# An encoder kernel on TensorE: where the first transposed piece of a step stands among the scores and the projection

## The reference

```python
h = rms_norm(x, g)
z = h @ w_in                       # q, k, v of both kinds of heads, and a gate
o = concat(diff_attention(...),    # 4 heads, each with two softmaxes over all 1024 keys
           neighbourhood_attention(...))   # 8 heads over an 8 x 16 neighbourhood
x = x + (o * silu(gate)) @ w_out
```

## Time and profile before

| what | value |
|---|---|
| time, median of 3 runs | 1527.56 us (1527.29 to 1528.21) |
| the profiled execution | 1533.38 us |
| its span | 1531.5 us |
| TensorE busy | 1458.8 us, 95% |
| VectorE busy | 908.7 us, 59% |
| ScalarE busy | 699.3 us, 46% |
| mean granted clock of TensorE | 0.98 of full speed |

### The profile page before, as it was taken

The page is one execution under the profiler, slowest core; times in us unless marked ns, Lnnn a source line. Parts: engine busy times, 40 slices in busy tenths (PEclk is TensorE's granted clock), DMA queues, the critical chain, the costliest instruction groups (busy, mean ns, idle before and its releaser), DMA issues. The chain is left out here.

```text
span 1531.5 us, 24892 instructions
## 1 busy us (share of the span) xinstructions
PE 1458.8 (95%) x8288; PEld 1192.9 (78%) x8288; DVE 908.7 (59%) x1892; ACT 699.3 (46%) x1338; POOL 507.3 (33%) x498
## 2 busy tenths in 40 slices
PE   7899999999999999899999999999999999997995
PEld 6687887878787878678887878788878888876874
DVE  6467676767555555663436766767665555557323
ACT  5345554555444444442515555545444444454330
POOL 2233333243423232302643242423252323331261
PEclk9899999999999999899999999999999999998996
DMA  6500101111111201301210111001111111122012
GB/s 197 119 29 22 48 21 34 34 44 50 36 52 42 58 34 58 131 15 42 69 42 28 36 35 34 21 31 37 53 42 53 42 51 41 51 70 82 28 55 110
DMA packets 39249, 79.45 MB, mean 52 GB/s; under 512 B 18832, under 2 KB 18832, under 8 KB 39184
## 3 DMA queue, kind: packets, MB, share of 16 engines
q1 hardware_dynamic: 39184, 78.60, 16.5%
HBM read 66.57 MB, written 15.96 MB: 54 GB/s over the span
## 5 line engine op out<-in xcount | busy, mean ns | idle before, releaser
L877 PE MATMUL proj<-h_hi,w_hi 128*128 128x512 f32 x1184 | 504.4, 426 | 31.0 <-DVE h_lo L1371 13.7
L879 PE MATMUL proj<-h_hi,w_lo 128*128 128x512 f32 x1184 | 469.6, 397 | 0.0
L878 PE MATMUL proj<-h_lo,w_hi 128*128 128x512 f32 x1184 | 466.4, 394 | 0.0
L877 PEld LDWEIGHTS proj<-h_hi,w_hi 128*128 128x128 f32 x1184 | 224.8, 190 | 106.5 <-issue 61.7
L879 PEld LDWEIGHTS proj<-h_hi,w_lo 128*128 128x128 f32 x1184 | 224.3, 189 | 52.3
L878 PEld LDWEIGHTS proj<-h_lo,w_hi 128*128 128x128 f32 x1184 | 225.9, 191 | 34.6
L1281 DVE CUSTOM_DVE_ANT_0 prob<-scores,inner 128x1024 f32<-128x1024 f32 (+1 forms) x192 | 204.2, 1063 | 50.0 <-PE scores L913 47.2
L1289 DVE TENSOR_TENSOR pt_lo<-turn,pt_hi 128x512 fp32r<-128x512 f32 (+1 forms) x208 | 138.8, 667 | 147.2 <-ACT pt_hi L746 146.7
L557 POOL TENSOR_TENSOR w_lo<-w_raw,w_hi 128x1024 fp32r<-128x1024 f32 x78 | 188.7, 2419 | 109.3 <-ACT w_hi L704 109.2
L746 ACT ACTIVATE pt_hi<-turn 128x512 fp32r<-128x512 f32 (+1 forms) x208 | 120.7, 580 | 225.0 <-PE turn L970 225.0
L772 ACT ACTIVATE prob<-prob,nm,escale_now 128x1024 f32<-128x1024 f32 x128 | 158.2, 1236 | 0.4 <-DVE nm L1285 0.4
(11 more groups left out here) (159 smaller groups left out, 2226.8 us busy)
## 6 DMA issues: line engine op xcount, KB each, us to landing
w_raw<-chunks SPq DMA_DIRECT2D x81, 512.0 KB, 3.4
mixed_dram<-gate SPq DMA_DIRECT2D x28, 256.0 KB, 2.3
edge<-bias_dram SPq DMA_DIRECT2D x32, 224.0 KB, 3.8
h_lo<-mixed_dram SPq DMA_DIRECT2D x14, 512.0 KB, 7.1
xt<-x_t SPq DMA_DIRECT2D x8, 512.0 KB, 9.4
bias_dram<-bias_rows SPq DMA_DIRECT2D x16, 240.0 KB, 6.1
out_t<-prob SPq DMA_DIRECT2D x6, 512.0 KB, 3.0
out_t<-gate SPq DMA_DIRECT2D x2, 512.0 KB, 3.0
```

Of the source, the lines that this page charges most:

```text
L877: pe.matmul(dst, a_hi, b_hi, start=start, stop=False)
L878: pe.matmul(dst, a_hi, b_lo, start=False, stop=False)
L879: return pe.matmul(dst, a_lo, b_hi, start=False, stop=stop)
```

## The change

TensorE's step: before, the piece of projection was cut into three parts of 2, 3 and 3 contraction steps, and the first transposed piece stood between the first two. Now the first transposed piece stands directly behind the scores, and the projection fills in parts of 5 and 3. In the last group of a layer the slots of `LAST_FILL` are taken two, one and one. VectorE's step in a DA group: the low part of the first piece now stands between the two `shifted`, not behind both. In an NA group VectorE's order stays; in the last group the additions of slot 0 move behind the first `p_part`.

```diff
-                    parts = [range(0, 2), range(2, 5), range(5, 8)]
-                    if last_step:
-                        parts = [range(0, 2), range(2, 5), range(5, 8), ()]
+                    parts = [range(0, 5), range(5, 8), ()]
 
                     def fill(j):
-                        if not behind and LAST_FILL[t] and j < len(LAST_FILL[t]):
-                            for p, ks in LAST_FILL[t][j]:
-                                out_piece(g.l, p, ks)
+                        if not behind:
+                            for slot in LAST_FILL[t][(0, 2, 3)[j]:(2, 3, 4)[j]]:
+                                for p, ks in slot:
+                                    out_piece(g.l, p, ks)
                         if front and front.projects(ft):
                             group_piece(front, ft, parts[j])
 
+                    turn_p(g, t - 1, 0)
                     fill(0)
-                    turn_p(g, t - 1, 0)
-                    fill(1)
                     turn_p(g, t - 1, 1)
                     if g.na and INNER[t - 1]:
                         turn_p(g, t - 1, 2)
-                    fill(2)
+                    fill(1)
...
             def attend(g, behind):
                 for t, front, ft in steps(g, behind):
-                    if front:
-                        for m in range(2):
-                            shifted(front, ft, m)
...
+                    if front:
+                        shifted(front, ft, 0)
+                    if not g.na:
+                        p_part(g, t - 1, 0)
+                    if front:
+                        shifted(front, ft, 1)
                     for c in range(3 if g.na and INNER[t - 1] else 2):
-                        if c < 2:
-                            add_pieces(c)
-                        p_part(g, t - 1, c)
+                        if c == 1:
+                            add_pieces(0)
+                            add_pieces(1)
+                        if g.na or c:
+                            p_part(g, t - 1, c)
```

More of the change, by code:

```diff
@@ L1072, in attend @@
                         turn_v(behind, 1, 2 if g.na else 1)
-                        fill(3)
                         score(behind, 1)
                     elif t == NT:
-                        fill(3)
+                        fill(2)
                     if t == NT and not g.na:
```

## The result

The changed kernel takes 1533.67 us (median of 7 runs, 1530.32 to 1536.19), the kernel before 1528.21 us in its 7 runs: a ratio of 1.0033, 95% interval 1.0024 to 1.0043. It is slower, by 5.0 us by this ratio and by 5.5 us by the two medians. I had forecast slower by 13.4 us. The sign is right and so is the mechanism at the seams, but the size is off by more than a factor of two.

A forecast was written before the change was run, and what follows sets the result against it. TensorE, busy 95% of the span, was taken to set the time. Terms 8.4 + 1.1 + 0.9 + 1.2 - 4 = +7.6 us, plus 6.8 for the clock less 1, gave +13.4 on 1527.56: 1541 us, range 1531 to 1549.

The forecast's parts named there:

- NA seams: Six places, NA group into NA group: TensorE idles until VectorE frees the piece's bank; 1.395 us each, +8.4 us.
- DA seams: Six places, DA group into DA group: the piece behind `turn_u` waits for its bank; +1.1 us (0 to 2.4).
- the last group: Step 6 of each layer's last group: additions move behind the first low part, TensorE waits; +0.6 us a layer, +1.2.
- Layer 1: First step of layer 1: TensorE waits for the piece's probabilities before the six products; +0.9 us (0 to 1.4).
- The ordinary step: 98 steps where the first piece and six products change places: 0.04 us gained each, -4 us (0 to -18).
- The clock: Seven new long stalls, four followed by half clock at 1.7 us each: +6.8 us, less 1 for stretches shifting away.
- Six products fall into the 1.35 us: First step of layer 2: the six products fall into the second piece's existing wait, so cost 0.
- B: Rival: seams stall but the clock holds, with none or one stretch of low clock; 1533 to 1536 us, chance 0.22.
- A: The forecast itself: seams stall, two or more followed by low clock; 1536 to 1549 us, likeliest 1541, chance 0.56.
- C: Rival: a switch cheaper by 0.1 us a step pays back the seams; about 1528 us, chance 0.12.
- D: Rival: the costly switch from scores to products goes altogether, 0.18 us a step; faster, 1521.5 us, chance 0.06.
- E: Rival: the switch from scores costs nothing in either order, so the 4 us go; 1545 us, chance 0.04.

The follow-up runs named there:

- experiment 3: The kernel before, with only the first piece in step 1 of the NA groups moved directly behind the scores: 1539.12 us, ratio 1.0056.
- Experiment 8: Changed kernel, with groups' first steps and last groups in TensorE's old order, one contraction step ahead of the first piece in ordinary steps: 1526.18 us, ratio 0.9979.
- experiment 9: The changed kernel itself, unaltered, profiled a second time: 1535.83 us, one execution.
- experiment 2: Changed kernel with step 1 of every group and the layers' last groups back in the old order, only ordinary steps changed: 1520.24 us, ratio 0.9939.

## Why the prediction was off

**What bounds the kernel; the seams.** Right. The NA seams were forecast at 1.395 us each and measured at 1.37 to 1.43 in the changed kernel, and alone in experiment 3 at 1.36 to 1.42 in the four places without half clock. DA seams (+1.1, measured +1.0) and the last group (+1.2, measured +1.05) hold too, and nothing that stalls is given back later. Layer 1 (+0.9) holds as far as it can be told: the +1.2 of the table have one more stretch of half clock in them, and at equal half clock it is 0.7 to 1.2.

**"The ordinary step": the term -4 us.** This step failed in size: it is -7.6. I took six products behind the block at 6 x 0.2325 = 1.395 us, with a spacing read over four intervals early in a run. In the long run the six add 3.53 - 2.17 = 1.36 us, 0.227 us each, which is the spacing at the end of such a run. And I took the block at 0.42 where it costs 0.41. With these the step comes to 2.17 - (0.33 + 0.41 + 1.36) = 0.07 us, as measured. I noted that rounding was as large as the result and multiplied by 98 all the same. Experiment 8 shows that the gain hangs on the switch from scores to products, as said; my bound of 0.18 us a step held.

**"The clock": the term +6.8 us, less 1.** This failed in size, too, and more: one of the seven new stalls of the changed kernel was followed by a stretch of half clock in two of its profiles, and two in the other, of experiment 9. I took four from the lengths of stalls alone. It is the stall at layer 2 each time, +1.4 us, and in experiment 9 one NA seam besides. No run shows the 1 us that I took off for stretches that shift away. With the other terms as forecast and this one as measured the sum is 9.0 us; with the ordinary step mended as well it is 5.4, and 5.0 is measured.

**"Six products fall into the 1.35 us" at layer 2: 0.** Right for the changed kernel but for the clock. That VectorE's new order removes this wait by itself (experiment 2) I had missed: I looked for what its change could delay, and not at the one place where the low part was late.

**The rivals.** The measured time is in B's range (seams stall, none or one stretch, 1533 to 1536 us), to which I gave 0.22, and not in A's. B's own sum, though, is 1534.2 to 1536.9 us; the time lies half a microsecond under it, which is less than its runs differ by. C asked for 0.1 us a step and D for 0.12 and more; it is 0.077. E (a switch that costs nothing) is refuted by the step's 0.075 us. The weight loads (PEld) fit that: behind the scores the first load starts with its product, at 306.69 for the product at 306.70, and in the run that follows each starts more than 0.2 us ahead of its own, as the one below at 307.04 for the product at 307.26.

```profile
306.69 0.19 PEld L877 LDWEIGHTS proj<-h_hi,w_hi 128*128 128x128 f32 x1 [0.36 <-issue]
...
307.04 0.19 PEld L879 LDWEIGHTS proj<-h_hi,w_lo 128*128 128x128 f32 x1
```

The Trainium skill (page "TensorE: Matmul & The Clock Gate", section "Step-by-step: what each phase is for") says that weight loads are pulled ahead of running matmuls where row groups don't conflict or the load goes to the background buffer. The run of products agrees, and the first load behind the half-height scores is a case where it doesn't happen; which of the two conditions fails there, no run shows.

## What to carry to other kernels

Move a waiting instruction ahead of filler only where its input is ready at the new place; one rule for all steps of a loop hides that the first step after a seam has other inputs. Here the same edit gains 0.5% (7.6 us) in the ordinary steps and loses more than that at the seams. With the filler sized for each place, and VectorE's new order, the kernel is 0.9% faster than before. When a term is hundredths of a microsecond times a hundred steps, measure it over a whole unbroken run of instructions, not from rounded neighbours. Don't price a change of clock by the length of a stall.

## What the hardware showed

Directly behind score products of 64 rows a block of four transposes takes 0.41 us, and 0.36 us behind full-height products: 0.05 us more. Six projection products take 1.49 us in that place and 1.36 us at the end of a long run, 0.13 us more. So the block is the cheaper neighbour. The spacing of projection products falls along a run, from 0.228 to 0.236 us behind its first distance to 0.227 us from the eighth product on (DA steps of the changed kernel). And stalls of 1.9 to 2.4 us were followed by a lower granted clock in 3 of 30 cases at one place, and stalls of 2.1 us in 6 of 6 at another.
